# A chunked RWKV-7 scan in a transformer kernel: both directions share the matrix array, and the block inverses are finished one step later

## The reference, cut to what matters

```python
def wkv_scan(r, w, k, v, a, b, s0, reverse):
    def step(s, inp):
        r_t, w_t, k_t, v_t, a_t, b_t = inp
        sa = jnp.einsum('bhvk,bhk->bhv', s, a_t)
        s = s * w_t[:, :, None, :] + sa[..., None] * b_t[:, :, None, :] + v_t[..., None] * k_t[:, :, None, :]
        return s, jnp.einsum('bhvk,bhk->bhv', s, r_t)
    ...
    s_final, ys = lax.scan(step, s0, xs, reverse=reverse)
    return s_final, jnp.moveaxis(ys, 0, 1)
```

## Time and profile before

| | |
|---|---|
| time before, median of 3 runs | 3985.72 us (3984.34 to 3987.25) |
| the profiled execution's own time | 3984.07 us |
| its span, first to last instruction | 3982.2 us |
| TensorE busy over the span | 3566.7 us (90%), mean granted clock 0.949 |
| VectorE / ScalarE / GpSimd busy | 2077.2 (52%) / 1535.0 (39%) / 230.5 us (6%) |
| the scan | from 1506.7 to 1965.4 us of the span, 458.7 us |
| TensorE / VectorE busy in the scan | 364.5 / 259.5 us |

### The profile page before, as it was taken

One profiled execution on the slowest core, in us unless ns is written; L12 is line 12 of the kernel. 1 busy time (PEld: TensorE's weight loads), 2 busy tenths in 40 slices (PEclk: granted clock), 3 DMA queues, 4 the chain that ended last, 5 costly groups with the idle time before them and its releaser, 6 DMA issues.

```text
span 3982.2 us, 59861 instructions
## 1 busy us (share of the span) xinstructions
PE 3566.7 (90%) x24692; PEld 2817.5 (71%) x24692; DVE 2077.2 (52%) x3394; ACT 1535.0 (39%) x2762; POOL 230.5 (6%) x447
## 2 busy tenths in 40 slices
PE   6877899999967886888889999979999999799999
PEld 4644478888855665788668887756888666568886
DVE  4355453334475644666354445774444655544445
ACT  4466542222244642233343332533333434443334
POOL 0011000000000102333310000000000000000000
PEclk9989999999989987999999999988999999899999
DMA  4011113332114536565422222111222121022221
GB/s 192 32 64 61 62 63 133 117 141 82 54 66 138 152 110 175 150 164 139 146 74 96 95 96 105 56 43 59 85 98 104 64 82 53 32 73 102 85 98 61
DMA packets 294206, 378.49 MB, mean 95 GB/s; under 512 B 240432, under 2 KB 243376, under 8 KB 259248
## 3 DMA queue, kind: packets, MB, share of 16 engines
q1 hardware_dynamic: 280560, 328.78, 25.6%
q10 hardware_dynamic: 13376, 45.88, 3.1%
HBM read 330.56 MB, written 44.06 MB: 94 GB/s over the span
## 4 chain that ended last, share of the span: by engine, by line
PE 73%; DVE 10%; ACT 7%; DMA 4%; issue 3%; POOL 2%; SPq 1%; ACTq 0%; DVEq 0%; POOLq 0%
PE ps L257 18%; PE ps L258 18%; PE ps L259 18%; PE ps L776 2%; DMA s_it<-rt 1%; PE ps L1271 1%; PE ps L1272 1%; PE ps L1273 1%; ACT s L807 1%; DVE mx L1571 1%; PE ps L339 1%; PE ps L766 1%; DVE wlo L249 1%; ACT whi L242 1%; POOL ri L2218 1%
## 5 line engine op out<-in xcount | busy, mean ns | idle before, releaser
L242 ACT ACTIVATE whi<-panel 128x512 fp32r<-128x512 f32 (+1 forms) x519 | 437.3, 843 | 577.2 <-PE ps L259 574.8
L249 DVE TENSOR_TENSOR wlo<-panel,whi 128x512 fp32r<-128x512 f32 (+1 forms) x519 | 498.5, 961 | 291.0 <-ACT whi L242 281.5
L257 PE MATMUL ps<-dh,whi 128*128 128x512 f32 (+1 forms) x1280 | 474.2, 370 | 0.0
L258 PE MATMUL ps<-dh,wlo 128*128 128x512 f32 (+1 forms) x1280 | 471.3, 368 | 0.0
L259 PE MATMUL ps<-dl,whi 128*128 128x512 f32 (+1 forms) x1280 | 471.0, 368 | 0.0
L257 PE MATMUL ps<-xh,whi 128*128 128x512 f32 x1088 | 443.1, 407 | 25.2 <-DVE xl L2533 18.8
L258 PE MATMUL ps<-xh,wlo 128*128 128x512 f32 x1088 | 429.2, 394 | 0.0
L259 PE MATMUL ps<-xl,whi 128*128 128x512 f32 x1088 | 428.8, 394 | 0.0
L257 PE MATMUL ps<-hh,whi 128*128 128x512 f32 (+1 forms) x960 | 351.8, 366 | 26.2 <-DVE hl L460 26.1
L258 PE MATMUL ps<-hh,wlo 128*128 128x512 f32 (+1 forms) x960 | 339.5, 354 | 0.0
L259 PE MATMUL ps<-hl,whi 128*128 128x512 f32 (+1 forms) x960 | 339.4, 354 | 0.0
(11 more groups left out here) (537 smaller groups left out, 5973.3 us busy)
## 6 DMA issues: line engine op xcount, KB each, us to landing
panel<-in_w SPq DMA_DIRECT2D x248, 1024.0 KB, 4.8
late<-s_fe ACTq DMA_DIRECT2D x16, 1024.0 KB, 7.6
late<-s_fe ACTq DMA_DIRECT2D x48, 256.0 KB, 5.7
s_fe<-x SPq DMA_DIRECT2D x37, 256.0 KB, 2.7
late<-s_fe ACTq DMA_DIRECT2D x8, 768.0 KB, 6.8
s_fe<-x SPq DMA_DIRECT2D x40, 128.0 KB, 2.1
s_ia<-panel SPq DMA_DIRECT2D x24, 128.0 KB, 3.1
s_ia<-gg SPq DMA_DIRECT2D x24, 128.0 KB, 2.9
```

The source lines that it names most:

```text
L242: e.activation(unit(u)[0][:, 0:kc, :], w, ACT.Copy).then_inc(*w_hi.up(u))
L249: e.tensor_tensor(lo[:, 0:kc, :], w, hi[:, 0:kc, :].bitcast(F32), SUB).then_inc(*w_lo.up(u))
L257: e.matmul(out, hi[:, k, :], xh, start=k == 0, stop=False)
L258: e.matmul(out, lo[:, k, :], xh, start=False, stop=False)
```

## The change

The computation stays the same; the following is moved.

- **Four quarters.** In direction 1 the head-to-quarter map is crossed for `q4`, `q5`, the first half of `x4`, `z` (both parts), `u` and the state part of `y` (now a segment of its own, `ys`), by `side(h, d)`. These segments are issued for both directions at once: for each pair of heads, direction 0 (two quarters) and then direction 1 (the other two). The second half of `x4` and `x5` still go direction by direction.
- **Inverses one step later.** q4, x4, q5 and x5 of chunk i run in step i, between z(i) and u(i), no longer in step i-1. The orders on all engines are new (below; ScalarE: z, gates, bt, b2(0), v(0, i+1), u, v(1, i+1), b2(1), the loads of chunk i+4, the values of i+3, y). VectorE makes `GS` ahead in `grown`, and its state update `s` comes last in the step.
- **SyncE.** `inverses(i+1)` is issued between the two `blocks_out` of chunk i+2; the loads are split into `loaded_t` (XT, before `gather(i+2)`) and `loaded_a` (XA, after it).
- **Banks and buffers.** The outputs get a fixed bank for each direction (banks 0 and 1), the rest takes turns over six. `BT` has three buffers for each direction instead of two. `CM` gets a second copy with its column halves exchanged for direction 1 (two small VectorE copies at the start), used as `CM[:, n % 2, :]`. The program is built with `dynamic_dma_scratch_size=1024`.

The diff, cut to its core. Lines taken out stand in the functions above where they are left out here.

```diff
...
+    BT = [[alloc(stW, [P, 16, CH], name="bt") for _ in range(3)] for _ in range(2)]
...
     def scan_order():
         for i in range(-2, NCH):
+            now, new, next_ = i >= 0, i + 2 < NCH, 0 <= i + 1 < NCH
             if new:
+                yield "g", (0,), i + 2, 4
+            if now:
+                yield "z", BOTHD, i, 1
+                yield "q4", BOTHD, i, 1
             if new:
+                yield "g", (1,), i + 2, 4
+            if now:
+                yield "x4", BOTHD, i, 2
+                yield "q5", BOTHD, i, 1
+            if new:
+                yield "bt", (0,), i + 2, 2
+                yield "bt", (1,), i + 2, 2
+            if now:
+                yield "x5", BOTHD, i, 1
+            if next_:
+                yield "v", (0,), i + 1, 2
+            if is_main(i):
+                yield "ys", BOTHD, i, 1
+            if now:
+                yield "u", BOTHD, i, 1
+            if next_:
+                yield "v", (1,), i + 1, 2
+            if 0 <= i < NCH - 1:
+                yield "s", (0,), i, 1
+                yield "s", (1,), i, 1
+            if is_main(i):
+                yield "y", (0,), i, 0
+                yield "y", (1,), i, 0
+    BOTHD = (0, 1)
     SEGS = list(scan_order())
+    STILES = [("y" if seg == "ys" else seg, d, i, k) for seg, ds, i, n in SEGS for d in ds for k in range(n)]
+    TURNS = [tile for tile in STILES if tile[0] != "y"]
+    SPLACE = {tile: n for n, tile in enumerate(TURNS)}
     def sbank(*tile):
-        return B[SPLACE[tile] % 8]
+        return B[tile[1]] if tile[0] == "y" else B[2 + SPLACE[tile] % 6]
     def sbank_free(e, *tile):
-        if SPLACE[tile] >= 8:
-            seg, d, i, k = STILES[SPLACE[tile] - 8]
-            if seg in ("bt", "v", "z", "y", "u"):
+        if tile[0] == "y":
+            if tile[2] > 4:
+                e.wait_ge(*sn_ac[tile[1]].at("y", tile[2] - 1, 0))
+        elif SPLACE[tile] >= 6:
+            seg, d, i, k = TURNS[SPLACE[tile] - 6]
+            if seg in ("bt", "v", "z", "u"):
                 e.wait_ge(*sn_ac[d].at(seg, i, k))
-            if seg not in ("bt", "v", "z", "y"):
+            if seg not in ("bt", "v", "z"):
                 e.wait_ge(*sn_dv[d].at(seg, i, k))
     def half(par):
...
...
+    def side(h, d):
+        return half(h % 2 ^ d)
...
+        def q(seg, i):
+            for d in range(2):
                 if seg == "q4":
+                    e.wait_ge(*sn_x[d].at("xa", i, 1))
                 else:
+                    e.wait_ge(*sn_dv[d].at("x4", i, 0))
+            for j in range(8):
+                for d in range(2):
+                    for h in (2 * j, 2 * j + 1):
+                        x = e.matmul(sbank(seg, d, i, 0)[side(h, d), j * CH:j * CH + CH],
+                                     GG[d][i % 3][half(h % 2), h, 0:CH], XA[d][half(h % 2), j, :], start=True, stop=True)
+                    if j == 7:
+                        x.then_inc(*sn_mm[d].up(seg, i))
+        def x4(i):
+            for d in range(2):
+                e.wait_ge(*sn_dv[d].at("q4", i, 0))
+            for j in range(8):
+                for d in range(2):
+                    for h in (2 * j, 2 * j + 1):
+                        x = e.matmul(sbank("x4", d, i, 0)[half(h % 2), j * CH:j * CH + CH],
+                                     XT[d][i % 2][side(h, d), j, :], QQ[d][side(h, d), j, :], start=True, stop=True)
+                    if j == 7:
+                        x.then_inc(*sn_mm[d].up("x4a", i))
+            for d in range(2):
                 for h in range(16):
+                    rows, col = side(h, d), h // 2 * CH
+                    x = e.matmul(sbank("x4", d, i, 1)[rows, col:col + CH], QQ[d][rows, h // 2, :],
+                                 XT[d][i % 2][rows, h // 2, :], start=True, stop=True)
...
+        def z(i):
+            for d in range(2):
+                e.wait_ge(*sn_ac[d].at("v", i, 1))
+            for j in range(8):
+                for d in range(2):
+                    ar, G, uv, xt = place(d, i)
+                    for h in (2 * j, 2 * j + 1):
+                        oth = half(1 - h % 2)
+                        x = e.matmul(sbank("z", d, i, 0)[side(h, d), j * CH:j * CH + CH], G[oth, h, 0:CH], uv[oth, h, :],
+                                     start=j == 0, stop=False)
+                    if j == 7:
+                        x.then_inc(*sn_mm[d].up("zv", i))
...
+            e.dma_start(LD[d][:, first - d:5 - d, :, :], FE[c, :, first:5, :, :]).then_inc(*sn_ld[d].up(i, by=16))
+        def load_v(d, i):
             if i > 1:
                 e.wait_ge(*sn_mm[d].at("v", i - 2, 1))
...
+            if part == "keys":
                 e.wait_ge(*sn_ac[d].at("em", i))
                 e.wait_ge(*sn_ld[d].at(i))
-                if i > 2:
-                    chunk_done(e, d, i - 3)
                 if i > 0:
                     e.wait_ge(*sn_mm[d].at("bt", i - 1))
                     e.wait_ge(*sn_ac[d].at("b2", i - 1))
                 e.tensor_tensor(bk[:, :, 0, :], gb, b, MUL).then_inc(*sn_dv[d].up("b", i))
-                e.tensor_tensor(ar[:, :, 0, :], ga, kk, MUL).then_inc(*sn_dv[d].up("a", i))
+                e.tensor_tensor(bk[:, :, 1, :], gb, k, MUL).then_inc(*sn_dv[d].up("k", i))
                 return
-            e.tensor_tensor(bk[:, :, 1, :], gb, k, MUL).then_inc(*sn_dv[d].up("k", i))
+            if i > 2:
+                e.wait_ge(*sn_mm[d].at("ys" if is_main(i - 3) else "z", i - 3))
+            e.tensor_tensor(ar[:, :, 0, :], ga, kk, MUL).then_inc(*sn_dv[d].up("a", i))
             if is_main(i):
                 e.tensor_tensor(ar[:, :, 1, :], gr, r, MUL).then_inc(*sn_dv[d].up("r", i))
             first, last = (down[:, :, 0], up[:, :, CH]) if d == 0 else (up[:, :, CH], down[:, :, 0])
...
+        def s(d, i):
+            S, g = SS[d], GS[d]
+            e.wait_ge(*sn_mm[d].at("s", i))
+            if is_main(i):
+                e.wait_ge(*sn_mm[d].at("ys", i))
             e.tensor_tensor(S[:, :, :], S[:, :, :], fl(sbank("s", d, i, 0)), ADD).then_inc(*sn_dv[d].up("s", i, 0))
+            e.wait_ge(*sn_dv[d].at("gs", i))
             e.wait_ge(*sn_dv[d].at("s", i, 0))
...
         for i in range(-3, NCH):
+            now, new, next_ = i >= 0, 0 <= i + 2 < NCH, i + 3 < NCH
             if new:
                 g(0, i + 2)
+            if 0 <= i < NCH - 1:
+                grown(0, i)
+                grown(1, i)
+            if next_:
+                gates(0, i + 3)
+            if now:
+                q(0, i, "q4")
+                q(1, i, "q4")
+            if next_:
+                gates(1, i + 3)
+            if new:
                 g(1, i + 2)
+            if now:
+                x4(i)
+                q(0, i, "q5")
+                q(1, i, "q5")
+            if next_:
+                tilde(0, i + 3, "keys")
+            if now:
+                x5(0, i)
+                x5(1, i)
+            if next_:
+                tilde(0, i + 3, "queries")
+            if now:
                 u(0, i)
                 u(1, i)
             if next_:
+                tilde(1, i + 3, "keys")
+                tilde(1, i + 3, "queries")
+            if 0 <= i < NCH - 1:
+                s(0, i)
+                s(1, i)
...
             for d in range(2):
                 if i > 0:
-                    e.wait_ge(*sn_x[d].at(i - 1))
+                    e.wait_ge(*sn_x[d].at("xa", i - 1, 1))
             e.dma_start(blocks(IR), RI[:, :, :]).then_inc(*sn_r.up("ir", i, by=16))
             e.wait_ge(*sn_po.at("rt", i))
             e.dma_start(blocks(IT), RT[:, :, :]).then_inc(*sn_r.up("it", i, by=16))
+        def loaded_t(i):
             e.wait_ge(*sn_r.at("it", i))
+            for d in range(2):
+                if i > 1:
+                    e.wait_ge(*sn_mm[d].at("u", i - 2))
+                for par in range(2):
+                    e.dma_start(XT[d][i % 2][side(par, d), :, :], heads((IT, IR)[d], d, par)).then_inc(
+                        *sn_x[d].up("xt", i, par, by=16))
+        def loaded_a(i):
             for d in range(2):
                 if i > 0:
                     e.wait_ge(*sn_mm[d].at("q5", i - 1))
                     e.wait_ge(*sn_dv[d].at("x4", i - 1, 0))
-                if i > 1:
-                    e.wait_ge(*sn_mm[d].at("u", i - 2))
                 for par in range(2):
                     e.dma_start(XA[d][half(par), :, :], heads((IR, IT)[d], d, par)).then_inc(
                         *sn_x[d].up("xa", i, par, by=16))
-                    e.dma_start(XT[d][i % 2][half(par), :, :], heads((IT, IR)[d], d, par)).then_inc(
-                        *sn_x[d].up(*((i,) if par else ("xt", i)), by=16))
...
+            new, next_ = 0 <= i + 2 < NCH, 0 <= i + 1 < NCH
+            if new:
                 blocks_out(0, i + 2)
+            if next_:
+                inverses(i + 1)
+            if new:
                 blocks_out(1, i + 2)
+            if next_:
+                loaded_t(i + 1)
+            if new:
```

(2 more changed lines are left out.)

334 lines of the change are left out of this document (148 added, 186 removed).

## The result

The changed kernel takes 3956.95 us (median of 4 runs, 3953.5 to 3961.49), the kernel before in the same series 3985.27: ratio 0.993, 95% interval 0.9917 to 0.9942. It is 28.3 us faster where 83.8 were forecast, and the range (3885 to 3950) missed it. The profiled execution took 3956.97 us.

A forecast was written before the change was run, and what follows sets the result against it. Two near-equal limits were taken to bound the scan: a closed GpSimd/SyncE ring and TensorE's work. Start, four context steps of 27.5, six main steps of 28.8 and the end saved 83.8 us: 3902 us, range 3885 to 3950.

The forecast's parts named there:

- Part 1, the ring: Round of GpSimd, landing inverses, loads, sending blocks and gather: opened by the new order, 27.5 us (bounds 23 to 28).
- Part 2, the pace: TensorE's segments in turns on four quarters: starts 15 ns apart instead of 29, 64 instructions in 1.0 us.
- rival C: Turns bring nothing on TensorE (a pair takes 1.86 us), the open ring alone: 3948 us, chance 0.12.
- B: TensorE can't keep the pace through a run of 64, a pair takes 1.6 us: 3930 us, chance 0.17.
- 6.0 us less: Saving in a main step from seven pairs of segments taking turns (z twice, q4, x4's first half, q5, ys, u).
- Part 3, the walk: Main step walked in the new order: products, waits, shape changes and an allowance, 28.8 us where 33.6 stood.
- v(1) covers u's copies: Late in a main step, TensorE's v(1), until 23.9, hides u's copies, so s follows until 25.9.
- What is moved at no cost: ScalarE's loads at step end, y stores, output loads, CM copies: covered; decays have 1.3 us to spare at the median.
- Start: Start of the scan: first q4 at 1559 for both directions (1557.8 and 1561.5 before), step 0 at 1556.4.
- End: Last two steps: step 10 22.2 us, step 11 18.2, 2 us for a lower clock; scan ends at 1881.6.
- D (traffic): Transfers stretch and replace the ring, so all ten steps take 32 us: 3939 us, chance 0.09.
- E: Slower: hand-overs to VectorE stay open and turns bring nothing, main step 43.3 us: 4053 us, chance 0.08.

The follow-up runs named there:

- e2: The changed kernel without turns (direction 0's products first, then direction 1's, instead of alternating), full loads: 3956.6 us.
- e6: The changed kernel with 320 products more (five instruction blocks), in turns of all four quarters, while TensorE waits for the first XA: 3961.7 us.
- e5: The changed kernel with loads of chunks 5 to 11 cut to an eighth and no turns of the two directions: 3928.9 us.
- e4: The changed kernel, turns kept, with loads of chunks 5 to 11 (decays, keys, values) cut to an eighth: 3930.4 us.
- e1: The changed kernel with 128 already satisfied waits added to TensorE's stream at its start of the scan: 3946.75 us.
- e9: The changed kernel without turns, keys issued behind ScalarE's first two exponentials and values behind bt: 3943.0 us.
- e17: The changed kernel with loads spread as in e7 and turns only in z's value part, the first half of x4 and ys: 3939.8 us.
- e13: As e9, with SyncE issuing the output loads only when q4 of step 11 is done: 3944.3 us.
- e8: As e7, with y of the step before put between the value and state parts of z: 3953.5 us.
- e7: The changed kernel with ScalarE's loads spread: keys behind its first two exponentials, values behind its copies of bt: 3946.5 us.

## Why the prediction was wrong, step by step

From the start of the scan, the forecast ran 159.7 us to the start of step 4, then 172.8 for six main steps and 42.4 to the end. Measured: 178.8, 192.8 and 58.8. The 55.5 missing us are 19.1 + 20.0 + 16.4. (The measured steps start at z, the walked ones at g(0), 2.1 us earlier; this moves 2.1 us from the first part to the second and changes nothing in the sum.)

- **Part 1, the ring: right that it opens, not in what follows.** Rounds take 28.5 us in context steps against 27.5, just outside the bounds of 23 to 28, and TensorE's wait for XT is gone. But the queue now waits for VectorE in each round, so the terms added up (GpSimd, landing, XT, gather) are not what sets its length. What is left without turns (ring, new order, banks together) is the whole gain: e2 is 29 us faster than the kernel before. No run takes these parts from one another.
- **Part 2, the pace: right in the instant, wrong in worth. This is the step that failed.** By the prediction's own rival C turns are worth 46 us of its sum; the runs give them nothing (3956.95 with and 3956.6 without, 3930.4 and 3928.9 with small loads). 64 instructions of both directions start in 1.0 us (60 in 1.15 with the last one's length), for 128 in a row (e6). That speaks against the floor of about 25 ns between starts and against the row-group rule, which the prediction weighed from the Trainium skill's "TensorE: Matmul & The Clock Gate", sections "Back-to-back issue gap" and "Packing small matmuls"; rivals B and C lose their reason. But C's consequence, that turns bring nothing, is what the runs show. The term "6.0 us less" for seven pairs was a little too large to begin with: a pair without turns has its starts in 1.69 us (e5), with turns in 0.94 (e4), 5.3 for seven. In e4 against e5 3.3 us of busy time are left of it (each stop adds the length of a last product), and 2.4 go to block stops and 1.2 to hand-overs.
- **Part 3, the walk.** 28.8 us for a main step (27.8 and 0.9 are 28.7); 29.1 where loads are small, with x4 waiting 1.3 us (6.7 in five times; 1.8 walked). That this number came out is in part luck, since the kernel without turns has 29.5. "v(1) covers u's copies" was wrong with turns: s waits up to 1.4 us for VectorE (3.7 us in four times). The walk had no term for the supply of instructions. It also set out from 33.6 us as the present main step, the shortest of five; their mean is 35.2.
- **"What is moved at no cost": wrong for ScalarE's loads.** This term was put at nothing; cutting the loads small gives 26.6 us, of which the kernel before has 13.2. I checked whether each load lands in time, not what it passes on its way. The loads of both directions now leave together at the end of a step and meet z and q4, TensorE's fastest stretch: 4.5 us a main step (33.6 to 29.1) with the fall of the clock behind the stops.
- **Start: wrong.** The first q4 came 63.7 us into the scan against 52.3. From the scan's first store it came 12.6 us later than in the kernel before: 7.2 since the gather took 10.3 us behind the loads of chunk 1, 1.1 in GpSimd, and 4.3 since XT and the gather now go ahead of XA (from the landing of the inverses to q4 10.1 us against 5.7; the forecast had 1.2 for both). The other wait for XA, 5.5 us in step 1, had no term. **End: wrong** by 16.4: step 10 took 29.0 us against 22.2 forecast, step 11 29.8 against 18.2, with 2 allowed for the clock. The output loads landed some 17 us ahead of their use, but they cost blocks, and step 10 ran at 0.76 of the clock. The forecast's "before 26.7" for step 10 was a misreading: that row runs from z of step 9 to z of step 10. Step 10 took 32.8 us, and steps 10 and 11 together 49.6, so the end got longer with the change and not shorter:
```profile
1915.80:1948.60 32.80, 24.95 (x715) 23.81 (x712) 11.33 (x19) 3.57 (x6) 11.49 (x21) 0.84 0.62 187
```
- **Rivals.** The measured time is nearest to C's 3948, for another reason. D (traffic) was near in mechanism: "engines stand idle between bursts" was true and beside the point, since it is during the burst that the block is needed. E did not happen.

Open: what makes the clock fall in step 0 in every version of the changed kernel (14 to 29 us at half clock, 6.8 in the kernel before), what sets the context round now, beyond that VectorE's masks stand in it, and how much of step 11 is hand-overs; moving the burst did not shorten it (27.6 us).

## What to carry to other kernels

Count instructions as a resource: products divided by 128 (each brings a weight load), times the 4.0 us that e6 measured for a block, is an estimate to set beside the engines' own work, here 6.4 blocks or some 26 us a main step; below about 31 ns a product, faster products in a row bought stops here. Ask also which engine the next segment waits for: what TensorE saves ahead of a wait for VectorE can be worth nothing, as at x4 here. When a load is moved, ask besides "does it land in time" what small transfer (a gather of blocks, a block of instructions) it will stand in front of, and look at that stretch's DMA share, not the stage's mean. And when the "issue" waits of an engine grow, number its instructions: stops at one remainder of 256 were the supply here.

## What the hardware showed that I had not expected

- TensorE stops at every 256th instruction if the next block isn't there: 4.0 us a block in a run (e6), up to 7.9 us behind a burst (2.6 us of use and a stop of 5.2 in step 8).
- 128 waits in a row became 64 instructions (e1), so a shift of the stream must be read from the trace.
- A stop of 4.4 us had 6.8 us at 1.2 GHz with it. In e9 and e17, with stops of at most 2.8 us in main steps, the clock there stayed full; in e13 stops of 1.9 to 2.7 us had 3.4 us at 1.2 GHz behind them, so the length of a stop alone doesn't tell.
- Shifting the stream by 64 instructions alone changed the median by about 10 us (3956.95 to 3946.75). Differences up to that size between versions that also shift the stream may be luck of position, e8 against e7 among them.
